# Two later attentions of a two-block network: mask, scale and extremum of the scores in one VectorE operation per head and token tile, and a third buffer for the scores

## The reference

```python
# layer 0, heads 0 to 7: window of 128 keys, with a sink
s = einsum(q, k) * (hd ** -0.5)          # hd = 64
s = where(mask, s, -inf)
p = softmax(concatenate([s, sink], -1))[..., :-1]
# layer 0, heads 8 to 15: each query sees the 64 keys that an index score picks
s = where(valid, einsum(q, kg) * scale, -inf);  p = softmax(s)
# layer 1, 16 heads: causal (one block of 256 keys)
s = where(ok, einsum(q, kg) * scale, -inf);     p = softmax(s)
o = einsum(p, v)
```

## Time and profile before

| | |
|---|---|
| median of 3 runs | 1961.59 us |
| profiled execution, its own time | 1969.38 us |
| its span | 1967.6 us |
| PE busy | 1847.6 us (94%) |
| DVE, ACT busy | 710.2 us (36%), 541.1 us (28%) |
| mean granted TensorE clock | 0.969 |

### The profile page before, as it was taken

The page is one execution under the profiler, slowest core; times in us unless marked ns, Lnnn a source line. Parts: engine busy times, 40 slices in busy tenths (PEclk is TensorE's granted clock), DMA queues, the critical chain, the costliest instruction groups (busy, mean ns, idle before and its releaser), DMA issues.

```text
span 1967.6 us, 24756 instructions
## 1 busy us (share of the span) xinstructions
PE 1847.6 (94%) x10198; PEld 1142.8 (58%) x10198; DVE 710.2 (36%) x1132; ACT 541.1 (28%) x714; POOL 34.3 (2%) x21
## 2 busy tenths in 40 slices
PE   6998989999999999999999999985899999889997
PEld 6785774443443443443444344374689887668996
DVE  3252322111111111111111111268756568665645
ACT  4342441111111111111111111234444444544442
POOL 0100120000000000000000000000000000000001
PEclk9999997999999999999999999996899999999999
DMA  8749599999999999999999999531135454324551
GB/s 331 296 175 342 197 384 383 410 428 429 429 428 428 428 429 429 428 429 428 429 429 428 429 427 429 229 128 43 65 139 203 171 198 165 129 79 156 184 204 39
DMA packets 96315, 587.14 MB, mean 298 GB/s; under 512 B 6990, under 2 KB 7204, under 8 KB 70660
## 3 DMA queue, kind: packets, MB, share of 16 engines
q1 hardware_dynamic: 94820, 581.25, 73.1%
q10 hardware_dynamic: 1440, 5.11, 0.8%
HBM read 585.30 MB, written 1.05 MB: 298 GB/s over the span
## 4 chain that ended last, share of the span: by engine, by line
PE 87%; DVE 5%; DMA 3%; ACT 3%; issue 1%; SPq 0%; DVEq 0%; ACTq 0%
PE bank L1059 33%; PE bank L1315 23%; PE bank L1334 12%; PE bank L1272 7%; PE bank L1344 3%; DMA ring<-in_ada_w 2%; PE bank L1306 2%; PE bank L1134 1%; ACT arena L808 1%; PE bank L1443 1%; PE bank L1327 1%; DVE sb_XN L2029 1%; PE bank L1119 1%; DVE sb_XN L2058 1%; DMA ring<-in_w_o 1%
## 5 line engine op out<-in xcount | busy, mean ns | idle before, releaser
L1315 PE MATMUL bank<-ring,arena 128*64 128x512 f32 x2048 | 455.3, 597 | 0.0
L1315 PEld LDWEIGHTS bank<-ring,arena 128*64 128x64 f32 x2048 | 141.8, 137 | 307.3 <-issue 307.3
L1059 PE MATMUL bank<-w_hi,arena_r 128*128 128x512 f32 (+1 forms) x784 | 257.2, 390 | 4.7 <-DVE arena_r L2017 2.8
L1334 PE MATMUL bank<-ring,arena 128*64 128x512 f32 x1024 | 226.8, 595 | 16.8 <-ACT arena L808 16.8
L499 DVE TENSOR_TENSOR w_lo<-ring,w_hi 128x4096 fp32r<-128x4096 f32 (+2 forms) x45 | 196.5, 4367 | 47.3 <-ACT w_hi L489 44.9
L489 ACT ACTIVATE w_hi<-ring 128x4096 fp32r<-128x4096 f32 (+2 forms) x45 | 158.9, 3573 | 34.9 <-DMA ring<-in_c_w_in 19.3
L1059 PEld LDWEIGHTS bank<-w_hi,arena_r 128*128 128x128 f32 x784 | 147.6, 188 | 35.4 <-DVE arena_r L2017 3.3
L806 ACT ACTIVATE arena<-arena,sb_tab 128x512 f32<-128x512 f32 x32 | 23.1, 722 | 510.5 <-DVE arena L1920 510.5
L1334 PEld LDWEIGHTS bank<-ring,arena 128*64 128x64 f32 x1024 | 72.5, 137 | 150.5 <-issue 144.9
L1895 DVE TENSOR_SCALAR arena<-sb_tab,sb_pos 128x64 f32<-128x64 f32 x66 | 13.7, 251 | 387.8 <-PE bank L1315 387.8
L1059 PE MATMUL bank<-XT_r,w_hi 128*128 128x256 f32 x512 | 147.1, 287 | 4.3 <-DVE arena_r L2139 4.3
(11 more groups left out here) (334 smaller groups left out, 2167.6 us busy)
## 6 DMA issues: line engine op xcount, KB each, us to landing
ring<-in_w_gate_up SPq DMA_DIRECT2D x128, 2048.0 KB, 13.1
ring<-in_w_down SPq DMA_DIRECT2D x64, 2048.0 KB, 15.3
ring<-in_mlp_w SPq DMA_DIRECT2D x32, 2048.0 KB, 8.3
ring<-in_ada_w SPq DMA_DIRECT2D x24, 2048.0 KB, 12.2
ring<-in_c_w_in SPq DMA_DIRECT2D x6, 2048.0 KB, 7.6
ring<-in_w_in SPq DMA_DIRECT2D x4, 2048.0 KB, 10.0
ring<-in_w_k SPq DMA_DIRECT2D x2, 2048.0 KB, 12.3
ring<-in_w_v SPq DMA_DIRECT2D x2, 2048.0 KB, 8.7
```

The costliest lines, as they stand in the source:

```text
L1059: mm = pe.matmul(out, st[a], mv[b], start=start and a + b == 0, stop=stop and a == 1, skip_group_check=True)
L1315: mm = pe.matmul(B[m][CAP * h:CAP * h + CAP, :], xe[:, 2 * j + kl, :], w[:, kl, m * D + h * HW:m * D + (h + 1) * HW], start=False, stop=(j ...
L1334: mm = pe.matmul(B[2][CAP * h:CAP * h + CAP, :], hT[:, c, CAP * j:CAP * j + CAP], w[:, c, h * HW:(h + 1) * HW], start=(j == 0 and c == 0), ...
```

## The change

The scaling, the mask and the row extremum become one `tensor_tensor_reduce` per head and token tile. It writes (score + mask) · (-1/8), the negated score, and the minimum of that, which is the negated maximum; its starting value is the negated sink or a constant. `exps` then reads the negated scores with scale -1. The sinks are negated once. SC becomes `SCORES` with three buffers of two heads each, unit u in buffer u mod 3: two where SC was, the third in the arena. The wait on the transposes thereby goes back one unit further, and front(u) also waits for exps(u-2), which frees the statistics. `exps` waits for the four reductions in place of the last small operation; only the fifth activation waits for that.

```diff
-for _kind, _per in (("sc", 2), ("s", 2), ("nm", 1), ("p", 2), ("pt", 2), ("pte", 2)):
+for _kind, _per in (("sc", 2), ("s", 4), ("p", 2), ("pt", 2), ("pte", 2)):
...
-        SC = XNf[:, 0:1536].rearrange("p (h n) -> p h n", h=4)
+        SCORES = {st: [XNf[:, 0:768].rearrange("p (h n) -> p h n", h=2), XNf[:, 768:1536].rearrange("p (h n) -> p h n", h=2),
+                       arn(a, 2 * step).rearrange("p (h n) -> p h n", h=2)[:, :, 0:3 * P]]
+                  for st, a, step in (("ab", 0, 3728), ("cc", 1536, 2048))}
...
             def exps(st, u):
-                act.wait_ge(*upto(st, "nm", u + 1))
+                act.wait_ge(*upto(st, "s", 4 * u + 4))
...
-                        act.activation(sc, sc, ACT.Exp, bias=att[:, 1, i:i + 1],
+                        sc = SCORES[st][u % 3][:, h, a:b]
+                        act.activation(sc, sc, ACT.Exp, bias=att[:, 1, i:i + 1], scale=-1.0,
...
                 if u < ATTNS[st][1]:
+                    act.wait_ge(*upto(st, "nm", u + 1))
...
-                        pe.wait_ge(*upto(st, "s", a - 3))
+                        pe.wait_ge(*upto(st, "s", 2 * a - 6))
...
+                if u >= 3:
+                    dve.wait_ge(*upto(st, "pt", 2 * u - 4))
                 if u >= 2:
-                    dve.wait_ge(*upto(st, "pt", 2 * u - 2))
+                    dve.wait_ge(*upto(st, "e", exps_of(st, u - 1)))
                 for h in range(2):
                     dve.wait_ge(*upto(st, "sc", 2 * u + h + 1))
-                    dve.scalar_tensor_tensor(sc[:, h, :], B[2 * (u % 2) + h][:, 0:3 * P], HD ** -0.5, mask, ALU.mult,
-                                             ALU.add).then_inc(sem("s"), 1)
-                dve.wait_ge(*upto(st, "s", 2 * u + 2))
-                dve.reduce_max(att[:, 0, c:c + 2], sc[:, :, 0:P], AX.X)
-                link(dve.reduce_max(att[:, 0, c + 2:c + 4], sc[:, :, P:3 * P], AX.X))
+                    least = nsink[:, 2 * u + h:2 * u + h + 1] if sink else 3e38
+                    for t, (a, b) in enumerate(((0, P), (P, 3 * P))):
+                        ins = dve.tensor_tensor_reduce(sc[:, h, a:b], B[2 * (u % 2) + h][:, a:b], mask[:, a:b],
+                                                       -HD ** -0.5, least, ALU.add, ALU.min,
+                                                       att[:, 1, c + 2 * t + h:c + 2 * t + h + 1])
+                        ins.then_inc(sem("s"), 1)
                 if sink:
-                    sk = sinkb[:, None, 2 * u:2 * u + 2].to_broadcast((P, TB, 2))
-                    mx = att[:, 0, c:c + 4].rearrange("p (t h) -> p t h", t=TB)
-                    link(dve.tensor_tensor(mx, mx, sk, ALU.max))
-                ins = dve.tensor_scalar(att[:, 1, c:c + 4], att[:, 0, c:c + 4], -1.0, None, ALU.mult)
-                if sink:
-                    link(ins)
-                    ins = dve.tensor_tensor(att[:, 3, c:c + 4].rearrange("p (t h) -> p t h", t=TB), sk,
-                                            att[:, 1, c:c + 4].rearrange("p (t h) -> p t h", t=TB), ALU.add)
-                ins.then_inc(sem("nm"), 1)
+                    dve.wait_ge(*upto(st, "s", 4 * u + 4))
+                    sk = nsink[:, None, 2 * u:2 * u + 2].to_broadcast((P, TB, 2))
+                    dve.tensor_tensor(att[:, 3, c:c + 4].rearrange("p (t h) -> p t h", t=TB),
+                                      att[:, 1, c:c + 4].rearrange("p (t h) -> p t h", t=TB), sk,
+                                      ALU.subtract).then_inc(sem("nm"), 1)
...
             dve.wait_ge(sem("sink_landed"), 16)
+            link(dve.tensor_scalar(nsink, nsink, -1.0, None, ALU.mult))
             split_lo(dve, "ab_out", 0)
```

More of the change, by code:

```diff
@@ L204 @@
 SHARES["e"] = [(st, exps_of(st, u)) for st, (u, _) in ATTNS.items()]
+SHARES["nm"] = [(st, sinks) for st, (_, sinks) in ATTNS.items()]
 for _kind, _per in (("mlp_zero", 4), ("mlp_h", 8), ("mlp_relu", 16), ("mlp_sq", 16), ("mlp_tt", 16), ("mlp_lo", 16)):
@@ L282, in build_program @@
         mrep = vec[:, :, 0:NCAND]
-        sinkb = stat[:, 48:56]
+        nsink = stat[:, 48:56]
         flag = stat[0:NCAND, 56:57]
@@ L562, in _ @@
                             sem("pos_landed"), 16)
-                    sp.dma_start(sinkb, A["ab_sinks_2"][0:1, :].to_broadcast((P, 8))).then_inc(sem("sink_landed"), 16)
+                    sp.dma_start(nsink, A["ab_sinks_2"][0:1, :].to_broadcast((P, 8))).then_inc(sem("sink_landed"), 16)
                     sp.dma_start(dft, dft_d.rearrange("(t p) n -> p t n", p=P)).then_inc(sem("dft_landed"), 16)
@@ L891, in exps @@
                         i = c + 2 * t + h
-                        sc = SC[:, 2 * (u % 2) + h, a:b]
-                        act.activation(sc, sc, ACT.Exp, bias=att[:, 1, i:i + 1],
+                        sc = SCORES[st][u % 3][:, h, a:b]
+                        act.activation(sc, sc, ACT.Exp, bias=att[:, 1, i:i + 1], scale=-1.0,
                                        accum_out=att[:, 2, i:i + 1]).then_inc(sem("e"), 1)
                 if u < ATTNS[st][1]:
+                    act.wait_ge(*upto(st, "nm", u + 1))
                     act.activation(att[:, 4, c:c + 4], att[:, 3, c:c + 4], ACT.Exp, bias=zero).then_inc(sem("e"), 1)
@@ L1442, in attend @@
                         for c in range(3):
-                            mm = pe.transpose(B[4 + h][:, c * P:(c + 1) * P], SC[:, n % 4, c * P:(c + 1) * P], ident)
+                            mm = pe.transpose(B[4 + h][:, c * P:(c + 1) * P], SCORES[st][u % 3][:, h, c * P:(c + 1) * P], ident)
                         mm.then_inc(sem("pt"), 1)
@@ L2023, in front @@
                 c = 4 * (u % 2)
-                sc = SC[:, 2 * (u % 2):2 * (u % 2) + 2, :]
+                sc = SCORES[st][u % 3]
+                if u >= 3:
+                    dve.wait_ge(*upto(st, "pt", 2 * u - 4))
                 if u >= 2:
-                    dve.wait_ge(*upto(st, "pt", 2 * u - 2))
+                    dve.wait_ge(*upto(st, "e", exps_of(st, u - 1)))
                 for h in range(2):
                     dve.wait_ge(*upto(st, "sc", 2 * u + h + 1))
-                    dve.scalar_tensor_tensor(sc[:, h, :], B[2 * (u % 2) + h][:, 0:3 * P], HD ** -0.5, mask, ALU.mult,
-                                             ALU.add).then_inc(sem("s"), 1)
```

## The result

| | before | after |
|---|---|---|
| median of the runs | 1965.09 us (4 runs, 1956.55 to 1970.24) | 1941.13 us (4 runs, 1935.94 to 1941.35) |
| ratio | | 0.9874, 95% interval 0.9838 to 0.9911 |
| profiled execution, its span | 1967.6 us | 1939.5 us |

A forecast was written before the change was run, and what follows sets the result against it. TensorE was busy 94% of the span; in the attentions, TensorE and VectorE waited on each other. Savings of 10.5 ("ab") plus 10.7 ("cc") made 21.2 us, taking median 1961.59 to 1940.4; range 1935 to 1953, saving 17 to 24.

The forecast's parts named there:

- "ab" start: Fronts 0 and 1 of attention "ab": index scores behind them wait for ScalarE and TensorE, so at most some 0.3 us.
- "ab" rounds 0 and 1: In "ab", where VectorE is filled: wait for transposes gone, front takes 2.0 us; 2.2 us saved a round, 4.4 together.
- "ab" t(2) to t(3): In "ab", transposes of unit 2 to those of unit 3: TensorE limits at its lower clock; 0.3 us saved.
- "ab" t(3) to t(6): In "ab", transposes of unit 3 to those of unit 6: 14.53 us becomes 9.6, 4.9 saved.
- "ab" tail: In "ab", transposes of unit 6 to the end of the last ot_lo: 7.23 us becomes 6.3, 0.9 saved.
- "cc" start: Start of attention "cc": weights(0) waits 3.5 us for exps(0), where two fronts took 4.4; 0.8 us saved.
- "cc" t(0) to t(5): In "cc", transposes of unit 0 to those of unit 5: 22.5 us becomes 5 x 3.24 = 16.2, 6.2 saved.
- "cc" t(5) to t(6): In "cc", transposes of unit 5 to those of unit 6: 4.98 us becomes 3.1, 1.8 saved.
- "cc" tail: In "cc", transposes of unit 6 to the end of the last ot_lo: 8.23 us becomes 6.3, 1.9 saved.
- the ring: In both attentions, TensorE and VectorE each wait for the other every round: VectorE idle 0.97 us, TensorE 1.14.
- F: VectorE's time on the four new operation-and-read pairs of a front: 1.6 us, low bound 1.38, high 2.42; before, 2.18.
- the signs: For being right: "cc" rounds 3.2 to 3.4 us, 1.14 idle gone, fronts 1.4 to 2.0, "ab" multiplications to MAX8 2.0.

The follow-up runs named there:

- the halves: Two runs: kernel before with only the third buffer, attentions 95.6 us (ratio 0.9939); changed kernel with two buffers, fused operation only, 92.9 us (0.9938).
- the filler: Kernel before plus idle TensorE matmuls, results unread, ahead of unit 6's transposes in both attentions; with two of them, attentions 106.2 us, ratio 0.9983.

## Why the prediction was right, and where its sizes were off

| term of the sum | predicted | measured |
|---|---|---|
| "ab" start | 0 (to 0.3) | 0.2 |
| "ab" rounds 0 and 1 | 4.4 | 5.5 |
| "ab" t(2) to t(3) | 0.3 | 0.9 |
| "ab" t(3) to t(6) | 4.9 | 4.9 |
| "ab" tail | 0.9 | 1.2 |
| "cc" start | 0.8 | 1.2 |
| "cc" t(0) to t(5) | 6.2 | 6.6 |
| "cc" t(5) to t(6) | 1.8 | 1.8 |
| "cc" tail | 1.9 | 2.2 |
| sum | 21.2 | 24.4 (rounded terms: 24.5) |

- The mechanism held: the ring, TensorE next at 3.24 a round (measured 3.17; the 3.24 ended with the profile's modelled end of the last matmul, which the next start does not wait for), VectorE behind it. It stands further behind than forecast, 0.9 us in a plain round where I had 0.1, since F was shorter. The run with one reduction more shows the order of the two; the halves show that it takes a shorter VectorE round by either way to get near 3.2.
- The term that was mis-sized is F. Predicted 1.6 with bounds 1.38 and 2.42, measured 1.12, below the low bound. The columns were right (0.22 for 128, 0.34 for 256 from start to start, predicted 0.20 and 0.33). Wrong was the read, which I took at 0.08 at the least, as MATCH_VALUE_LOAD; it starts with the next operation and costs nothing. The scalar per partition was nearly right (0.06 an operation, predicted 0.05). F's error shows where VectorE is the bound: of the 1.1 us that "ab" rounds 0 and 1 gave more than forecast, F's part is 2 x 0.48. In the plain rounds of "cc" it hides. Two of the signs that the prediction gave for being right were sized by it and did not come: 1.4 to 2.0 us a front, and 2.0 us between the multiplications and MAX8 (1.47).
- That "ab" t(2) to t(3) gave 0.9 and not 0.3 is the clock, which rose in that step; in three other runs (the fused operation alone, one reduction more, ot_lo behind the multiplications) it rose later and the step took 5.18 or 5.19, next to no gain on the 5.24 before. The forecast's step was right for a clock as before, and the range named the other.
- The tails: right in cause. I put the clock's part by extrapolation at 6.3 a tail, and the filler in the kernel before measured it at 6.03.
- That the saving arrives whole: shown by the stretch between the attentions, 295.4 us in both, and the one from the last ot_lo to the end, 224.4 before and 223.0 after.
- The total came nearer (1940.4 against 1941.1) than the terms, and that is luck. The forecast started from a median of 1961.59 for the kernel before; with a fourth run of 1970.24 that median is 1965.09, 3.5 us higher, and this made up for a saving forecast 3.2 us too small. By the ratio the saving is 24.8, in the profile 24.4, where I had 21.2; both lie just above the 17 to 24 that I gave for the saving.
- The estimate from the Trainium skill (Vector Engine (DVE) Microarchitecture Reference, "5.2 Measured stream behaviour"), F = 1.40 with 75 ns for each of eight instructions, is too high by 0.28, which is the four reads at 0.07: for the four large operations it holds (1.10 by it, 1.12 measured). The rule against fusing (the Trainium skill, VectorE: DVE Perf Modes, "Rules for kernel authors") did not decide here: eight instructions took 1.12 us where five took 2.18. The rule of the Trainium skill on half rate (the same Reference, "7. Points that are easy to get wrong") had no case here, since one source is in PSUM; no run shows it.

## What to carry to other kernels

Where two engines wait for each other in a ring, look first for the sum of each one's own work per round. Here the larger of the two (TensorE's, with its short wait for ScalarE's copy) was what the cures could reach, and a further buffer and a shorter operation competed for the same idle time (13.8 and 16.5 us alone, 24.4 together), while in a stage that one engine filled they added. TensorE's idle time can have a second price, its clock on the work behind it (1.2 and 2.2 us in two tails here). It went when two idle matmuls filled that time, and in the runs where the time shrank to 1.54 us or less; at 1.73 to 1.87 us it went in one tail of four. Once an engine is no longer the bound, moving work off it pays only in the stages where it still is.

## What the runs showed of the hardware that was not expected

Three groups of line L2037 of the changed kernel: the 64 reads, operations of "cc" without a scalar per partition, and operations of "ab" with one, the sink (shortest, median and longest in ns; the shortest are those of 128 columns, the longest those of 256):

```profile
L2037 DVE DVE_READ_ACCUMULATOR2_ANT sb_att<- x64: 81/83/85, 1338.1 to 1708.6; 128x1 f32 x64
L2037 DVE CUSTOM_DVE_ANT_0 sb_XN<-bank,sb_tab x24: 285/356/421, 1686.9 to 1708.2; 128x128 f32<-128x128 f32 x12, 128x256 f32<-128x256 f32 x12
L2037 DVE CUSTOM_DVE_ANT_0 sb_XN<-bank,sb_tab,sb_stat x12: 344/415/481, 1337.8 to 1364.5; 128x128 f32<-128x128 f32 x6, 128x256 f32<-128x256 f32 x6
```

The read of VectorE's accumulator has a duration of 83 ns and adds none from start to start: in 56 of the 64 the next operation starts in the same nanosecond, and the other 8 have a wait or a gap before theirs. ScalarE's read adds 0.09 us: in the kernel before, the exponential that starts at 1715.07 has its read at 1715.37 and the next exponential at 1715.47. A scalar per partition adds 60 ns (285 to 344, 421 to 481). An idle float32 matmul of 512 columns is two instructions and 0.9 us at the full clock, which made the fillers of five and four too long by more than half. And a step of "ab" with the same instructions ahead of it and in it took 4.37 us in two profiles of the changed kernel and 5.19 in the one with ot_lo moved further on, by when TensorE's clock rose; that step's time is not to be read from one profile.
